# First weight units loaded and multiplied by k-tile, second block opened with two units, last norm's weights applied ahead

## What is computed

```python
x = x + 0.5 * swiglu(rmsnorm(x, ffn1_norm), ffn1_w_gu, ffn1_w_down)      # D_FF = 2816
x = x + token_mixing(rmsnorm(x, mix_norm), w_in, lb, hg_norm, conv_w, conv_norm, w_out)
x = x + cross_attention(rmsnorm(x, xa_norm), rmsnorm(mem, mem_norm), xa_wq, xa_wkv, xa_wo)
x = x + 0.5 * swiglu(rmsnorm(x, ffn2_norm), ffn2_w_gu, ffn2_w_down)
return rmsnorm(x, final_norm)

def rmsnorm(x, g):      return x * rsqrt(mean(x * x) + 1e-6) * g
def swiglu(h, gu, dn):  gate, up = split(h @ gu); return (silu(gate) * up) @ dn
```

## Time and profile before

| what | value |
|---|---|
| median of three runs | 1172.21 us |
| the profiled execution's own time | 1170.22 us |
| its span, from the first to the last instruction | 1168.4 us |
| PE busy | 1141.2 us, 98% of the span |
| POOL, DVE, ACT busy | 48%, 40%, 37% of the span |
| DMA | 113.10 MB, mean 97 GB/s |

### The profile page before, as it was taken

The page is one execution under the profiler, slowest core; times in us unless marked ns, Lnnn a source line. Parts: engine busy times, 40 slices in busy tenths (PEclk is TensorE's granted clock), DMA queues, the critical chain, the costliest instruction groups (busy, mean ns, idle before and its releaser), DMA issues.

```text
span 1168.4 us, 14941 instructions
## 1 busy us (share of the span) xinstructions
PE 1141.2 (98%) x5366; PEld 948.6 (81%) x5366; DVE 471.4 (40%) x660; ACT 429.2 (37%) x576; POOL 560.1 (48%) x412
## 2 busy tenths in 40 slices
PE   7999999999999999999999999999999999999997
PEld 4888888888888788888777888888888888888886
DVE  8332233222222568788567224455322322321112
ACT  6332232232223545554346543345223223222221
POOL 5544554555555333233435873145445445455550
PEclk9999999999999999999999999999999999999999
DMA  6323222323223221221222542123232232233312
GB/s 231 106 91 107 96 90 101 103 91 106 99 104 108 90 72 55 73 73 54 82 91 87 182 157 71 53 72 109 90 108 90 90 108 90 90 108 108 108 55 72
DMA packets 33317, 113.10 MB, mean 97 GB/s; under 512 B 3712, under 2 KB 5888, under 8 KB 33152
## 3 DMA queue, kind: packets, MB, share of 16 engines
q1 hardware_dynamic: 33136, 111.53, 27.5%
q10 hardware_dynamic: 144, 1.05, 0.2%
HBM read 110.47 MB, written 2.10 MB: 96 GB/s over the span
## 4 chain that ended last, share of the span: by engine, by line
issue 39%; PE 33%; POOL 27%; POOLq 0%; DVE 0%; ACT 0%; DVEq 0%
POOL wl L341 27%; PE bank L967 11%; PE bank L965 11%; PE bank L966 11%; DVE x L957 0%; POOLq L339 0%; POOLq L337 0%; PE n_bank L1008 0%; PE o_bank L1094 0%; ACT rstd L591 0%; PE o_bank L1095 0%; DVE x L952 0%; PE n_bank L1094 0%; PE n_bank L1095 0%; ACT rstd L592 0%
## 5 line engine op out<-in xcount | busy, mean ns | idle before, releaser
L341 POOL TENSOR_TENSOR wl<-raw,wh 128x512 fp32r<-128x512 f32 x408 | 559.9, 1395 | 582.1 <-ACT wh L353 305.9
L965 PE MATMUL bank<-xh,wh 128*128 128x512 f32 x952 | 375.2, 394 | 0.0
L967 PE MATMUL bank<-xh,wl 128*128 128x512 f32 x952 | 370.8, 389 | 0.0
L966 PE MATMUL bank<-xl,wh 128*128 128x512 f32 x952 | 370.5, 389 | 0.0
L366 ACT ACTIVATE wh<-raw 128x1024 fp32r<-128x1024 f32 x104 | 110.3, 1061 | 396.1 <-DVE ubuf L679 219.4
L966 PEld LDWEIGHTS bank<-xl,wh 128*128 128x128 f32 x952 | 178.8, 188 | 38.3 <-issue 1.7
L965 PEld LDWEIGHTS bank<-xh,wh 128*128 128x128 f32 x952 | 178.7, 188 | 38.2 <-issue 1.7
L967 PEld LDWEIGHTS bank<-xh,wl 128*128 128x128 f32 x952 | 178.7, 188 | 37.7
L353 ACT ACTIVATE wh<-raw 128x1024 fp32r<-128x1024 f32 x99 | 104.3, 1054 | 139.1 <-PE bank L967 137.9
L965 PE MATMUL bank<-hid_h,wh 128*128 128x512 f32 (+1 forms) x374 | 141.0, 377 | 0.0
L967 PE MATMUL bank<-hid_h,wl 128*128 128x512 f32 (+1 forms) x374 | 140.8, 377 | 0.0
(11 more groups left out here) (209 smaller groups left out, 1066.3 us busy)
## 6 DMA issues: line engine op xcount, KB each, us to landing
raw<-w_all SPq DMA_DIRECT2D x204, 512.0 KB, 3.2
x<-x_t SPq DMA_DIRECT2D x8, 256.0 KB, 4.3
out_t<-x SPq DMA_DIRECT2D x8, 256.0 KB, 2.3
memf<-mem_t ACTq DMA_DIRECT2D x1, 1024.0 KB, 4.9
gbuf<-masks_d SPq DMA_DIRECT2D x1, 256.0 KB, 7.9
ident<-ident_d SPq DMA_DIRECT2D x1, 64.0 KB, 7.4
par<-params SPq DMA_DIRECT2D x1, 36.5 KB, 3.1
```

The costliest lines, as they stand in the source:

```text
L341: ins = nc.gpsimd.tensor_tensor(wl[:, c, half], raw[:, c, half], wh[:, c, half].bitcast(f32), SUB)
L965: nc.tensor.matmul(out_, a[0], b_[0], start=first, stop=False)
L966: nc.tensor.matmul(out_, a[0], b_[1], start=False, stop=False)
L967: return nc.tensor.matmul(out_, a[1], b_[0], start=False, stop=last)
```

## The change

Seven edits, in the order of the program:

1. **Loads.** The first four units are no longer loaded one after another. Piece k is the 128 columns of k-tile k of all four units (4 x 512 bytes in each partition, 256 KB). ACT's queue issues pieces 0 and 1 at its very start. SP issues x tile 0, the parameters, x tile 1, piece 2, x tile 2, piece 3 and so on to piece 7 and x tile 7.
2. **High and low parts.** ACT makes the wh of pieces 1 to 7, DVE that of piece 0 and the wl of all eight; POOL starts with unit 4. Squares and their additions are put between them.
3. **PE.** Eight matmuls of ones by ones, 128 columns each, come first; their output is overwritten. Then for each k-tile 0 to 5 four wh·xh, four wh·xl and four wl·xh, into the four banks in turn. Then `sum_squares`, then for each unit the last two k-tiles.
4. **ACT before unit 4.** `ahead(u0)`, the wh of unit 4, stands behind the inverse root instead of ahead of it in the first feed-forward, and the function table for it is not loaded a second time.
5. **Second feed-forward.** PE runs seven k-tiles of unit 0, seven of unit 1, then the last k-tile of both, then `sum_squares`.
6. **Last norm.** ACT multiplies x tiles 0 to 6 by the last norm's gain behind their squares. The last multiplication is then three DVE operations of 128x2x256, one of 128x256 and, for tile 7 alone, the old one with the gain.
7. **Last sum.** The matmul of ones by `acc` no longer waits for the last square.

```diff
-            for m in range(KC):
-                sp.dma_start(x[:, m, :], x_t[m, :, :]).then_inc(x_loaded[m], 16)
-            for u in range(1, SLOTS):
-                sp.dma_start(raw[:, u, :], w_all[u, :, :]).then_inc(raw_loaded[u], 16)
+            for k in range(KC):
+                sp.dma_start(x[:, k, :], x_t[k, :, :]).then_inc(x_loaded[k], 16)
+                if k == 0:
+                    sp.dma_start(par[:, :], params).then_inc(par_loaded, 16)
+                if k + 1 >= 2 and k + 1 < KC:
+                    sp.dma_start(raw[:, :, 128 * k + 128:128 * k + 256],
+                                 w_all[0:SLOTS, :, 128 * k + 128:128 * k + 256].rearrange("u p n -> p u n"))\
+                      .then_inc(piece_loaded[k + 1], 16)
...
-                act.wait_ge(raw_loaded[slot], (u // SLOTS + 1) * 16)
-                if u >= SLOTS:
-                    act.wait_ge(unit_used, u + 1 - SLOTS)
+                act.wait_ge(raw_loaded[slot], u // SLOTS * 16)
+                act.wait_ge(unit_used, u + 1 - SLOTS)
...
-                        ahead(u0)
+                        if which == 1:
+                            ahead(u0)
                         inverse_root(norm, rstd[:, :], n_bank[:, :], D)
+                        if which == 0:
+                            ahead(u0)
                         act.wait_ge(group_read, g0 + 2 * j + 5)
                         nc.scalar.activation(gbuf[:, j, :], gbuf[:, j, :], ACT.Silu).then_inc(silu_ready, 1)
...
                         if m < KC - 1:
                             new_x(phase, m, qn, False)
-
+                            nc.scalar.activation(x[:, m, :], x[:, m, :], ACT.Copy, scale=pcol("final", m))\
+                                .then_inc(x_gain, 1)
...
+            for k in range(2):
+                ks = slice(128 * k, 128 * k + 128)
+                act.dma_start(raw[:, :, ks], w_all[0:SLOTS, :, ks].rearrange("u p n -> p u n"))\
+                   .then_inc(piece_loaded[k], 16)
             act.preload_act_table_set("natural_log_exp_and_others")
...
-            for m in range(KC):
-                act.wait_ge(x_loaded[m], 16)
-                nc.scalar.activation(xh[:, m, :], x[:, m, :], ACT.Copy, scale=pcol("ffn1", m)).then_inc(x_hi, 1)
-
-            act.wait_ge(hi_ready, 1)
-            hi(1)
-            for m in range(KC):
-                if m in (2, 5):
-                    hi(2 + m // 4)
-                square(x[:, m, :], Q_X0 + m)
+            for k in range(KC):
+                ks = slice(128 * k, 128 * k + 128)
+                if k > 0:
+                    act.wait_ge(piece_loaded[k], 16)
+                    ins = nc.scalar.activation(wh[:, :, ks], raw[:, :, ks], ACT.Copy)
+                    if k < KC - 1:
+                        ins.then_inc(piece_hi, 1)
+                    else:
+                        ins.then_inc(hi_ready, SLOTS)
+                act.wait_ge(x_loaded[k], 16)
+                nc.scalar.activation(xh[:, k, :], x[:, k, :], ACT.Copy, scale=pcol("ffn1", k)).then_inc(x_hi, 1)
+                if k > 0:
+                    square(x[:, k - 1, :], Q_X0 + k - 1)
+            square(x[:, KC - 1, :], Q_X0 + KC - 1)
...
-            dve.wait_ge(raw_loaded[0], 16)
-            V_.tensor_copy(wh[:, 0, :], raw[:, 0, :]).then_inc(hi_ready, 1)
+            dve.wait_ge(piece_loaded[0], 16)
+            V_.tensor_copy(wh[:, :, 0:128], raw[:, :, 0:128]).then_inc(first_hi, 1)
...
                         update_x(m, gd, U_DOWN2, 0.5, None, len(DOWN_SPLIT))
                         chunk_lo(4, m, Q_X4, None, False)
 
-            for m in range(KC):
-                dve.wait_ge(x_hi, m + 1)
-                V_.scalar_tensor_tensor(out=xl[:, m, :], in0=x[:, m, :], scalar=pcol("ffn1", m),
-                                        in1=xh[:, m, :].bitcast(f32), op0=MULT, op1=SUB).then_inc(x_lo, 1)
-            for m in range(KC):
+            for k in range(KC):
+                ks = slice(128 * k, 128 * k + 128)
+                if k == 0:
+                    dve.wait_ge(first_hi, 1)
+                elif k < KC - 1:
+                    dve.wait_ge(piece_hi, k)
+                else:
+                    dve.wait_ge(hi_ready, SLOTS)
+                ins = V_.tensor_tensor(wl[:, :, ks], raw[:, :, ks], wh[:, :, ks].bitcast(f32), SUB)
+                if k < KC - 1:
+                    ins.then_inc(piece_lo, 1)
+                else:
+                    ins.then_inc(lo_ready, SLOTS)
+                dve.wait_ge(x_hi, k + 1)
+                V_.scalar_tensor_tensor(out=xl[:, k, :], in0=x[:, k, :], scalar=pcol("ffn1", k),
+                                        in1=xh[:, k, :].bitcast(f32), op0=MULT, op1=SUB).then_inc(x_lo, 1)
+                if k > 1:
+                    add_squares(Q_X0 + k - 2)
+            for m in range(KC - 2, KC):
                 add_squares(Q_X0 + m)
             dve.wait_ge(lb_exp, 1)
             link(V_.tensor_tensor(lbs[:, 3, :], lbs[:, 1, :], lbs[:, 2, :], ADD))
...
-                    xs = x[:, m, HALVES[h]]
-                    V_.scalar_tensor_tensor(out=xs, in0=xs, scalar=pcol("final", m), in1=rstd[:, HALVES[h]],
-                                            op0=MULT, op1=MULT).then_inc(cat_new, 1)
+                dve.wait_ge(x_gain, KC - 1)
+                inv = rstd[:, HALVES[h]]
+                for m in range(0, KC - 2, 2):
+                    xs = x[:, m:m + 2, HALVES[h]]
+                    V_.tensor_tensor(xs, xs, inv.rearrange("p (a t) -> p a t", a=1).to_broadcast([128, 2, T // 2]), MULT)\
+                        .then_inc(out_new, 1)
+                xs = x[:, KC - 2, HALVES[h]]
+                V_.tensor_tensor(xs, xs, inv, MULT)
+                xs = x[:, KC - 1, HALVES[h]]
+                V_.scalar_tensor_tensor(out=xs, in0=xs, scalar=pcol("final", KC - 1), in1=inv,
+                                        op0=MULT, op1=MULT).then_inc(out_new, 1)
 
...
-                    pe.wait_ge(hi_ready, 1)
-                    for k in range(KC):
+                    pe.wait_ge(group_read, SLOTS)
+                    for k in range(KC - 2):
+                        if k == 0:
+                            pe.wait_ge(first_hi, 1)
+                        else:
+                            pe.wait_ge(piece_hi, k)
                         pe.wait_ge(x_hi, k + 1)
-                        nc.tensor.matmul(bank[0][:, :], wh[:, 0, 128 * k:128 * k + 128], xh[:, k, :],
-                                         start=(k == 0), stop=False)
-                    pe.wait_ge(lo_ready, 1)
-                    for k in range(KC):
+                        for c in range(SLOTS):
+                            nc.tensor.matmul(bank[c][:, :], wh[:, c, 128 * k:128 * k + 128], xh[:, k, :],
+                                             start=(k == 0), stop=False)
                         pe.wait_ge(x_lo, k + 1)
-                        nc.tensor.matmul(bank[0][:, :], wh[:, 0, 128 * k:128 * k + 128], xl[:, k, :],
-                                         start=False, stop=False)
-                        last = nc.tensor.matmul(bank[0][:, :], wl[:, 0, 128 * k:128 * k + 128], xh[:, k, :],
-                                                start=False, stop=(k == KC - 1))
-                    last.then_inc(unit_used, 1)
-                    group(u0 + 1, g0 + 1)
+                        for c in range(SLOTS):
+                            nc.tensor.matmul(bank[c][:, :], wh[:, c, 128 * k:128 * k + 128], xl[:, k, :],
+                                             start=False, stop=False)
+                        pe.wait_ge(piece_lo, k + 1)
+                        for c in range(SLOTS):
+                            nc.tensor.matmul(bank[c][:, :], wl[:, c, 128 * k:128 * k + 128], xh[:, k, :],
+                                             start=False, stop=False)
                     sum_squares(norm, qn + KC)
+                    pe.wait_ge(lo_ready, SLOTS)
+                    pe.wait_ge(x_lo, KC)
+                    for c in range(SLOTS):
+                        for k in range(KC - 2, KC):
+                            last = product(bank[c][:, :], wpair(c, 128 * k, 128 * k + 128),
+                                           (xh[:, k, :], xl[:, k, :]), False, k == KC - 1)
+                        last.then_inc(unit_used, 1)
                 else:
-                    group(u0, g0, x_phase=ph)
+                    for ks in (range(KC - 1), range(KC - 1, KC)):
+                        for c in range(2):
+                            pe.wait_ge(lo_ready, u0 + c + 1)
+                            pe.wait_ge(group_read, g0 + c + 1)
+                            for k in ks:
+                                pe.wait_ge(x_lo, KC * ph + k + 1)
+                                last = product(bank[(g0 + c) % 4][:, :], wpair((u0 + c) % SLOTS, 128 * k, 128 * k + 128),
+                                               (xh[:, k, :], xl[:, k, :]), k == 0, k == KC - 1)
+                            if k == KC - 1:
```

(10 more changed lines are left out.)

19 lines of the change are left out of this document (11 added, 8 removed).

## The result

The changed kernel has a median of **1163.36 us** over four runs (1161.14 to 1164.55); the kernel before, with four runs beside it, 1172.35 us (1170.49 to 1172.49). The ratio is **0.9925 (0.9913 to 0.9937)**, 9.0 us less. The profiled execution of the change took 1163.28 us with a span of 1161.5; that of before had 1170.22 and 1168.4. The forecast was 1164.4 us for the median, and 1162.4 with a span of 1160.5 for the profiled execution.

A forecast was written before the change was run, and what follows sets the result against it. PE, busy 98% of the span, was taken to bound the kernel. Start 7.3, less 0.2 at unit 4, plus 0.75 at the end, made 7.85 us; from the median of 1172.21 this gave 1164.4 us, range 1161.0 to 1168.6.

The forecast's parts named there:

- PE's own time: Start, 72 matmuls from P to S: 16.4 us at full rate, plus 1.1 for 5.5 slow matmuls and 0.4 for waits.
- When PE begins: Start of the kernel: PE's first product after piece 0 lands and is cast, at 5.3 us (4.7 to 5.8).
- S: New start time of the first feed-forward's sum of squares on PE: 23.2 us, bounds 21.8 and 25.5.
- P: Time at which PE begins its first product at the kernel's start: 5.3 us, bounds 4.7 and 5.8.
- start gain: How much earlier unit 4 starts on PE, 30.5 - S: 7.3 us (5.0 to 8.7), before 0.2 lost at unit 4.
- ACT and DVE: Start, preparing k-tiles: ACT 1.9 us each, DVE 1.9 to 2.1; DVE's additions allow S no earlier than 22 to 23.6 us.
- Rival B: Start: ACT and DVE set S, at 2.7 us per k-tile S = 27.1, gain 4.0, time 1168.2 us; chance 0.14.
- The loads: First 16 us: 512-byte rows at 290 GB/s, 1.7 us per k-tile against PE's 2.7, so loads stay ahead.
- Rival C: Loads of the first 16 us: slow 512-byte rows make it slower, decided from 107 GB/s down; 1175.9 us at 90; chance 0.04.
- Unit 4: Behind the first sum of squares: low part ready after 6.1 us, PE wants it at 6.4; wait 0 to 0.5, 0.2 us lost.
- Last half: End of the kernel: 0.44 us gained from last square to Ln, 0.3 at the multiplications, together 0.75 us (0.5 to 1.3).
- Rival A: Start: clock high from the first real matmul, S = 22 by DVE, gain 8.5, time 1163.2 us; chance 0.15.

The follow-up runs named there:

- the repeat: The changed kernel run once more with no edit: 1163.66 us over six runs, ratio 0.9926 to the kernel before.

## Why the prediction was right, and where its steps were not

The forecast of 1164.4 us is 1.0 above the first median and 0.7 above the repeat; both lie well inside 1161.0 to 1168.6. The mechanism of the start was right: PE's own time sets it, DVE and the loads keep ahead. Step by step:

- **When PE begins:** forecast 5.3 us with bounds 4.7 and 5.8, measured 5.66. Piece 0 was ready at 5.02, nearly as reckoned. What came later, high part of x tile 0, stood on the parameters' load, which the working had only as a competitor for bandwidth and not as something that the first product waits for. With the parameters first it is x tile 0 that comes as late (4.78 us). The first product needs both loads beside piece 0, and the last of the three counts.
- **PE's own time, the term that was mis-sized:** "I take half of the slow ones, 5.5 matmuls" gave S = 23.2 us. In the profiled execution 11.3 matmuls ran at 0.426 us (5.66 to 10.48), S = 24.32: 0.36 us from the later begin, 1.15 from 5.8 more slow matmuls, and 0.4 less for waits inside the first k-tile that did not come. In the repeat none was slow, and S was 22.46. The two ends of the working, 23.8 and 21.7 from P = 5.3, were both real: the same kernel does the one or the other. Without ones about 14 matmuls were slow, where the working's upper end had 10.5. Half of it was the mean of two cases that each happen, not a case. The start gain was 6.28 us in the one trace and 8.14 in the other, around the 7.1 forecast. The Trainium skill (TensorE: Matmul & The Clock Gate, Part 1) says that the number of matmuls at the low clock varies from run to run of one kernel; 11.3 and none agree.
- **ACT and DVE:** forecast ready at 22 to 23.6 us on DVE, measured 21.2: with POOL silent the additions stayed at 0.68 us, as assumed, and k-tile 1 was done at about 8.0 us, not 9.5. 1.87 us per k-tile is the lower end of the 1.9 to 2.1. Rival B falls.
- **The loads:** 290 GB/s assumed for rows of 512 bytes, 288 measured by their packets, 311 to 340 together with the x tiles at a full share, and PE waits for no later piece. Rival C falls: its point of decision was 107 GB/s.
- **Unit 4:** 0.2 us lost by the forecast, none measured, with the low part finished 0.13 us ahead of PE. S to unit 4 is 6.34 us for the 6.4 reckoned.
- **Second feed-forward:** 0 us, as forecast, shown by the trace and by the kernel without that edit. **Gains ahead:** no wait came of them.
- **Last half:** 0.75 us forecast, 0.7 measured; of it 0.44 between square and Ln exactly as reckoned, and 0.3 at the multiplications. These got 0.62 us shorter and the end only 0.3 earlier, with the stores at a full share (1.02, 339 GB/s), as said.
- **Rival A,** the clock high from the first real matmul, is what happened in the repeat and with ten ones. Its price was near, start gain 8.1 for 8.5, but not its bound: DVE was done at 21.2 us there and PE itself set the sum at 22.46. It was a chance of each execution and not of the kernel, and at 0.15 it was put low: two of the four profiles with eight ones show it.

The span came out at 1161.5 for 1160.5, 1.0 us longer than forecast, and the median at 1163.4 for 1164.4, 1.0 shorter: the two errors have opposite signs. The medians moved by 9.0 us and the traces by 6.9, where 7.85 was forecast for both. That the median came out so near is partly luck: S alone differs by 1.9 us between two executions of the kernel, and stretches of 1.6 us come and go. The profiled execution of before lay 2.1 us under its median, a little more than one stretch of lower clock costs, and that of the change at its median. The old start seems to have a place for such a stretch that the prediction didn't see. The traces of the two other kernels with the old start (the last norm alone, the ones in the kernel before) have one at 25.03 and 26.38 us, at the end of PE's wait for DVE ahead of the sum of squares or just behind it, and reach unit 4 at 38.73 and 38.80 us, 1.8 to 1.9 later than the profiled execution of before, 1.4 to 1.6 of it behind the sum. None of the nine traces with the new start, where PE doesn't wait there, has one. So against an execution with this stretch the change saves about 1.5 us more than the pair of profiles shows. The other executions of before have only their times (1170.3 to 1175.4 us): that many of them had this stretch is the likely reason, not a shown one.

## What to carry to other kernels

At the start of a kernel, order the work so that each landed piece feeds as many matmuls as it can: the new start was worth 5.7 us in the trace without ones (36.94 to 31.25 for unit 4), and the ones in the old start nothing. Warming matmuls belong into waits that are there anyway, no more of them than the wait holds, and into those later waits of TensorE behind which traces show the clock falling. Before comparing two traces, list the stretches at the lower clock in both: here each of those in the mixing part is worth 1.5 to 1.6 us, more than the two edits at the end together brought (0.7), and the one at 628 us nothing.
